# Moving the sample part of an RWKV-7 recurrence into the last round of its prompt part

## What is computed

```python
def step(S, inp):
    r_t, d_t, k_t, v_t, kk_t, b_t = inp
    sk = jnp.einsum('bhvk,bhk->bhv', S, kk_t)
    S = S * d_t[:, :, None, :] - sk[..., None] * b_t[:, :, None, :] + v_t[..., None] * k_t[:, :, None, :]
    return S, jnp.einsum('bhvk,bhk->bhv', S, r_t)
...
sT, y = lax.scan(step, s0.astype(f32), ...)
```

## Time and profile before

| | us |
|---|---|
| median of 3 runs | 4527.35 (4520.64 to 4532.71) |
| the profiled execution | 4527.17 |
| its span, first to last instruction | 4525.6 |

### The profile page before, as it was taken

How to read it: one execution, slowest core, us unless ns; L and a number is a source line. 1 busy time by engine, 2 the same in 40 slices (tenths; PEclk the granted TensorE clock), 3 DMA queues, 4 the chain that set the end, 5 groups by cost and what they waited for, 6 DMA issues and landing times. The chain is left out here.

```text
span 4525.6 us, 85734 instructions
## 1 busy us (share of the span) xinstructions
PE 4238.1 (94%) x32575; PEld 3841.0 (85%) x32575; DVE 3222.4 (71%) x6005; ACT 1430.4 (32%) x2183; POOL 1565.4 (35%) x1316
## 2 busy tenths in 40 slices
PE   7989998998777998999999998999999999999997
PEld 4888887887654987978888887999999999999996
DVE  5631334554655236899995664999999999999997
ACT  2211322111545123233336775222222222222223
POOL 6333334554022110034442332443434343443430
PEclk9999999998767999999999999999999999999998
DMA  4655665455352321134444445999999999999994
GB/s 170 204 185 191 207 231 185 178 202 169 94 172 81 89 112 52 38 104 145 142 144 158 179 172 189 344 302 299 302 298 302 302 300 302 300 302 298 304 298 156
DMA packets 523006, 928.01 MB, mean 205 GB/s; under 512 B 284032, under 2 KB 351232, under 8 KB 518688
## 3 DMA queue, kind: packets, MB, share of 16 engines
q1 hardware_dynamic: 387024, 549.29, 37.0%
q0 software_dynamic: 80960, 346.96, 22.4%
q10 hardware_dynamic: 54816, 28.85, 2.2%
HBM read 785.79 MB, written 206.30 MB: 219 GB/s over the span
## 5 line engine op out<-in xcount | busy, mean ns | idle before, releaser
L3258 POOL DMA_INDIRECT ex_rows<-expert_rows,ex_here x512 | 585.7, 1144 | 950.4 <-DVE acc_tok L3393 860.6
L3393 DVE SCALAR_TENSOR_TENSOR acc_tok<-ex_rows,ex_wsp,acc_tok 128x1024 f32<-128x1024 f32 x512 | 633.6, 1278 | 0.0
L2637 PE MATMUL ex_psa<-x_dense_high,eg_u_high 128*128 128x288 f32 x2048 | 604.4, 295 | 13.9 <-DVEq L3447 13.9
L2728 POOL TENSOR_TENSOR eg_u_low<-eg_u,eg_u_high 128x1024 fp32r<-128x1024 f32 x130 | 329.1, 2532 | 807.8 <-ACT eg_u_high L2723 807.8
L2637 PE MATMUL ex_psa<-x_dense_low,eg_u_high 128*128 128x288 f32 x2048 | 604.4, 295 | 0.0
L2637 PE MATMUL ex_psa<-x_dense_high,eg_u_low 128*128 128x288 f32 x2048 | 604.0, 295 | 0.0
L3290 PE MATMUL ex_pso<-ex_w_high,ex_v_high 128*128 128x288 f32 x2048 | 441.2, 297 | 9.7 <-DVE acc L3375 7.8
L3290 PE MATMUL ex_pso<-ex_w_high,ex_v_low 128*128 128x288 f32 x2048 | 439.9, 297 | 0.0
L3290 PE MATMUL ex_pso<-ex_w_low,ex_v_high 128*128 128x288 f32 x2048 | 438.6, 296 | 0.0
L3321 ACT ACTIVATE ex_w<-ex_psa 128x288 f32<-128x288 f32 x256 | 105.2, 411 | 1054.6 <-PE ex_psa L2637 1054.5
L3375 DVE TENSOR_TENSOR acc<-ex_pso,acc 128x576 f32<-128x576 f32 x512 | 373.8, 750 | 47.1 <-PE ex_pso L3290 47.1
(11 more groups left out here) (528 smaller groups left out, 9602.3 us busy)
## 6 DMA issues: line engine op xcount, KB each, us to landing
eg_u<-in_u SPq DMA_DIRECT2D x256, 512.0 KB, 5.4
expert_rows<-in_v SPq DMA_DIRECT2D x128, 512.0 KB, 7.0
ex_v<-in_v SPq DMA_DIRECT2D x128, 512.0 KB, 6.6
weights<-wt_stage SPq DMA_DIRECT2D x9, 4096.0 KB, 12.2
ex_g<-weights SPq DMA_DIRECT2D x128, 288.0 KB, 7.0
expert_rows<-eg_act SPq DMA_DIRECT2D x256, 128.0 KB, 1.7
proj<-in_out POOLq DMA_DIRECT2D x50, 548.5 KB, 6.2
in_w<-in_w_in SPq DMA_DIRECT2D x50, 512.0 KB, 4.7
```

The costliest lines, as they stand in the source:

```text
L2637: yield nc.tensor.matmul(out[:, 0:b - a], w[:, kc, :], half[:, kc, a:b], start=n == 0, stop=n == len(passes) - 1)
L2728: self.k.nc.gpsimd.tensor_tensor(self.ul[par][:, :, :], self.u[par % 2][:, :, :], self.uh[par][:, :, :].bitcast(F32), ALU.subtract).then_i ...
L3258: pool.indirect_dma_start(rows[i][:, :], None, table, index(here[par][:, t, j:j + 1]), element_offset=ROW_RUNS[t][0]).then_inc(s_row[i], 16)
L3393: v.scalar_tensor_tensor(out=acc_tok[:, t, :], in0=rows[i][:, at:at + D], scalar=wsp[:, i:i + 1], in1=acc_tok[:, t, :], op0=ALU.mult, op1= ...
```

## The change

`phase_rw_samples` is gone. Its work is split over the last round of `phase_rw_prompt` and what stands behind it in the same block:

- The matrix part of the sample chunk takes the place of "the next round's matrix parts" in the last round, on TensorE, ScalarE and VectorE. It uses the banks of `rwc_ps` that a chunk 0 uses and the buffers of the chunk set that the last round leaves free.
- The masking of the inputs is cut in 4 instructions of 128 x 1024, one after each piece of VectorE (`sample_inputs_masked`), with a semaphore of its own.
- The sample's state part follows the last round on each engine. In y, the product with the states comes first and the wait for u stands in the first head only; the mask of the values (half of `um`) is made ahead of rhs, and `um` lies over the conditioning weights' buffers.
- The last round's conditioning matmuls now wait for the sample chunk's `t0` step, since it shares their bank.
- One block boundary and its waits for stores are gone; two small VectorE instructions (L161 in the rows, the scaled gains) stand behind the sample part.

```diff
+class RwSampleBuffers:
...
+        self.chunk, self.ps, self.rhs, self.u = chunk, b.ps, b.rhs, b.u
...
+        self.y = ctx.enter_context(k.nc.sbuf_tensor("rws_y", [P, NPAIR, CL], F32))
+        self.kr = ctx.enter_context(k.nc.sbuf_tensor("rws_kr", [P, 2 * NPAIR, NSEQ, CL], F32))
...
+        bs = RwSampleBuffers(k, ctx, b, b.sets[R % 2][0], levels)
+        um = nc.alloc_sbuf_tensor_at("rws_um", [P, 2, NPAIR, NSEQ, CL], dtype=F32, offset=ada_at)
+        KR_PIECES = 4
+        BANK_YS, SBANK = 2, (0, 1, 3, 4)
...
+                sp.wait_ge(bs.AC.sem, bs.AC.done("y_0"))
+                sp.dma_start(io["rw_y"][NCH], bs.y[:, :, :]).then_inc(s_out, 16)
+                sp.wait_ge(bs.DV.sem, bs.DV.done("s_0"))
+                sp.dma_start(io["wkv_out"][1:NCOND].rearrange("s p a v -> p s a v"), rws.S[:, :, :, :]).then_inc(s_out, 16)
...
                         else:
                             since(pe, DS, "mod_1", r - 1)
-                            since(pe, DV, "t0_1", min(r + 1, R - 1))
+                            if r + 1 < R:
+                                since(pe, DV, "t0_1", r + 1)
+                            else:
+                                pe.wait_ge(bs.DV.sem, bs.DV.done("t0_0"))
...
+                def sample_matrix_part():
+                    pe.wait_ge(rws.s_in, 32)
+                    since(pe, AS, "y_1", R - 2)
+                    since(pe, DS, "mod_1", R - 2)
+                    since(pe, AC, f"mx{LEVELS - 1}_1", R - 1)
+                    since(pe, DV, f"t{LEVELS - 1}_1", R - 1)
+                    yield from rw_matrix_pe(k, bs, bs.chunk, rws.in5, levels, wait_of(pe))
+
+                def sample_state_part():
...
+                    at(bs.AC, "tok")
+                    pe.wait_ge(bs.s_kr, KR_PIECES)
...
+                    mm.then_inc(*bs.PE.inc("u_0"))
+                    pe.wait_ge(DS.sem, DS.done("mod_1", R - 1))
+                    for p_, rows in heads:
+                        o_ = four(BANK_YS)[rows, p_, :]
+                        for s in range(NSEQ):
+                            nc.tensor.matmul(o_, St[rows, s, p_, :], kr[rows, NPAIR + p_, s, :], start=s == 0, stop=False)
+                        nc.tensor.matmul(o_, ch.tok[rows, 2, p_, :], ch.mt[rows, p_, 192:256], start=False, stop=False)
+                        if p_ == 0 and rows.start == 0:
+                            at(bs.AC, "u")
...
                 for r in range(R):
-                    in_turn([state_part(r)] + (matrix_parts(r + 1) if r + 1 < R else []))
+                    in_turn([state_part(r)] + (matrix_parts(r + 1) if r + 1 < R else [sample_matrix_part()]))
+                sample_state_part()
...
+                def sample_inputs_masked():
+                    dve.wait_ge(rws.s_in, 32)
+                    n = 2 * NPAIR // KR_PIECES
...
+                    for i in range(0, 2 * NPAIR, n):
+                        v.tensor_tensor(bs.kr[:, i:i + n, :, :], bc(src[:, i:i + n], [P, n, NSEQ, CL]),
+                                        bc(k.seq_cols[:, :, :].unsqueeze(1), [P, n, NSEQ, CL]), ALU.mult).then_inc(bs.s_kr, 1)
+                        yield
...
-def phase_rw_samples(k, rws):
...
-                v.tensor_tensor(kr[:, :, :, :], bc(src, [P, 2 * NPAIR, NSEQ, CL]),
-                                bc(k.seq_cols[:, :, :].unsqueeze(1), [P, 2 * NPAIR, NSEQ, CL]),
-                                ALU.mult).then_inc(*DV.inc("masked_0"))
...
                 phase_rw_prompt(k, rws, ssd)
-                phase_rw_samples(k, rws)
```

More of the change, by code:

```diff
@@ L1156, in __init__ @@
         self.DV = Progress(k.sem(f"{tag}_dve"), *in_turn_steps(chunks, ["mt", "t0", "xy0"], [["t", "xy"]], levels), *each(after_dve))
+class RwSampleBuffers:
+    def __init__(self, k, ctx, b, chunk, levels):
+        self.chunk, self.ps, self.rhs, self.u = chunk, b.ps, b.rhs, b.u
+        after = lambda *steps: [f"{s}_0" for s in steps]
+        self.PE = Progress(k.sem("rws_pe"), *in_turn_steps((0,), ["mt", "m", "tok"], [["mx"], ["xmx"]], levels),
+                           *after("rhs", "u", "y", "s"))
+        self.AC = Progress(k.sem("rws_act"), *in_turn_steps((0,), ["tok"], [["mx"]], levels), *after("u", "y"))
+        self.DV = Progress(k.sem("rws_dve"), *in_turn_steps((0,), ["mt", "t0", "xy0"], [["t", "xy"]], levels),
+                           *after("rhs", "umask", "s_add", "s"))
+        self.s_kr = k.sem("rws_inputs_masked")
+        self.y = ctx.enter_context(k.nc.sbuf_tensor("rws_y", [P, NPAIR, CL], F32))
+        self.kr = ctx.enter_context(k.nc.sbuf_tensor("rws_kr", [P, 2 * NPAIR, NSEQ, CL], F32))
 class RwSampleInput:
@@ L1237, in phase_rw_prompt @@
         R = NCH // 2
+        levels = DSEQ.bit_length() - 1
+        bs = RwSampleBuffers(k, ctx, b, b.sets[R % 2][0], levels)
+        um = nc.alloc_sbuf_tensor_at("rws_um", [P, 2, NPAIR, NSEQ, CL], dtype=F32, offset=ada_at)
+        KR_PIECES = 4
+        BANK_YS, SBANK = 2, (0, 1, 3, 4)
+        s_out = k.sem("rws_stored")
+        wait_of = lambda eng: (lambda S_, step: eng.wait_ge(S_.sem, S_.done(step)))
         def at_of(eng, r):
@@ new lines, in sample_state_part @@
+                def sample_state_part():
+                    ch, St = bs.chunk, rws.S
+                    at = lambda S_, step: dve.wait_ge(S_.sem, S_.done(f"{step}_0"))
+                    rows_of = bc(k.seq_rows[:, :].unsqueeze(1).unsqueeze(3), [P, NPAIR, NSEQ, CL])
+                    dve.wait_ge(DS.sem, DS.done("mod_1", R - 1))
+                    at(bs.AC, "tok")
+                    v.tensor_tensor(um[:, 1], bc(ch.tok[:, 2, :, :].unsqueeze(2), [P, NPAIR, NSEQ, CL]), rows_of, ALU.mult)
+                    at(bs.PE, "rhs")
+                    v.tensor_copy(bs.rhs[:, :, :], four(BANK_U)).then_inc(*bs.DV.inc("rhs_0"))
+                    at(bs.AC, "u")
+                    v.tensor_tensor(um[:, 0], bc(bs.u[:, :, :].unsqueeze(2), [P, NPAIR, NSEQ, CL]), rows_of,
+                                    ALU.mult).then_inc(*bs.DV.inc("umask_0"))
+                    at(bs.PE, "s")
+                    for p_ in range(NPAIR):
+                        last = v.tensor_tensor(St[:, :, p_, :], b.ps[:, SBANK[p_], :].rearrange("p (s t) -> p s t", s=NSEQ),
+                                               St[:, :, p_, :], ALU.add)
+                    last.then_inc(*bs.DV.inc("s_add_0"))
+                    at(bs.DV, "s_add")
+                    for p_ in range(NPAIR):
+                        last = v.tensor_tensor(St[:, :, p_, :], St[:, :, p_, :],
+                                               bc(k.lam_end[:, p_, NCH:NCH + NSEQ].unsqueeze(2), [P, NSEQ, CL]), ALU.mult)
+                    last.then_inc(*bs.DV.inc("s_0"))
@@ L1453, in _ @@
+                sample_parts = lambda: [rw_matrix_dve(k, bs, bs.chunk, 1, levels, wait_of(dve)), sample_inputs_masked()]
                 in_turn(matrix_parts(0))
                 for r in range(R):
[L1455 removed]
+                    in_turn([state_part(r)] + (matrix_parts(r + 1) if r + 1 < R else sample_parts()))
+                sample_state_part()
                 dve.wait_ge(DS.sem, DS.done("mod_1", R - 1))
```

126 lines of the change are left out of this document (33 added, 93 removed).

## The result

| | before | after |
|---|---|---|
| median, one session | 4525.44 us (5 runs) | 4487.48 us (5 runs, 4481.52 to 4497.46) |
| ratio | | 0.9927, 95% interval 0.9909 to 0.9945 |
| median, a second chip | 4518.62 us (32 runs, 4496.24 to 4533.42) | 4489.18 us (9 runs, 4481.1 to 4500.45) |
| ratio | | 0.9943, 0.9924 to 0.9961 |
| span of the profiled execution | 4525.6 us | 4485.9 us |

The kernel became faster by 0.6 to 0.7%, clearly more than 0.3%, the least that can be told from no change. The forecast of 4510 and its range from 4500 to 4518 are both missed, on the fast side.

A forecast was written before the change was run, and what follows sets the result against it. It took the way from the prompt's last round to the Mamba-2 block as what counts, since everything behind starts at a block boundary. 19.97 - 5.7 + 0.6 + 2.1 = 17.0 us off 4527.35 gave 4510, range 4500 to 4518.

The forecast's parts named there:

- Removed, 19.97 us: Boundary, inverse and masking leave the path between the last round's matmuls and the sample's rhs: 19.97 us saved.
- Added, 5.7 us: Sample inverse and masking pieces put into the last round lengthen it by 5.7 us, 4 to 12 at the ends.
- The head: First piece of the sample's inverse, between rhs and the conditioning matmuls of the last round: 3.0 us added.
- The levels: The inverse's levels, matmuls on TensorE in the last round, with 0.3 of wait for a mask: 2.2 us added.
- the second rhs: In the last round, VectorE does a level and a masking piece before copying the second rhs: 0.55 us added.
- rival C: A single chunk's uncovered waits and masking pieces stretched beside GpSimd: 11.0 us saved, 4516; chance 0.22.
- rival D: Slower: pauses drop the clock to 1.2 GHz through the last round, 24.7 against 20.6 us removed, 4531; chance 0.02.
- The second half stays at 1.2 GHz, the pause before the second u gets no shorter: Last round from u on: clock left as it was, so no saving counted there.
- The clock, 2.1 us: The sample's rhs starts at 2.4 GHz and keeps it for about 3 us only: 2.1 us saved.
- the 0.6 for y's wait: In the sample part, y's first matmuls no longer wait for u's copy: 0.6 us saved.
- rival B: The clock holds at 2.4 GHz through the sample's rhs and y: 26 us saved, 4501; chance 0.18.
- Which stretch falls on which side of a clock change may move by a microsecond or two: Phases behind the edit start as before relative to the change, shifting by only a microsecond or two.

The follow-up runs named there:

- again: The kernel before, or the changed kernel, run once more unchanged for a second trace; medians 4519.25 us (before) and 4489.18 us (changed).
- x11: The kernel before with two more zeroings of `sp_state` ahead of the Mamba-2 prompt part; 4515.64 us, ratio 1.0000 to the kernel before.
- x12: The kernel before with five more zeroings of `sp_state` ahead of the Mamba-2 prompt part; 4517.63 us, ratio 1.0004 to the kernel before.
- x9: The changed kernel with two more zeroings of `sp_state` ahead of the Mamba-2 prompt part; 4488.76 us, ratio 0.9940 to the kernel before.
- x10: The changed kernel with five more zeroings of `sp_state` ahead of the Mamba-2 prompt part; 4491.78 us, ratio 0.9939 to the kernel before.
- x7: The changed kernel with the wait for the sample states' store moved into the Mamba-2 block; 4487.01 us, ratio 0.9940 to the kernel before.
- x4: The changed kernel with the sample's inverse and masks behind the last round, not interleaved with it; 4510.43 us, ratio 0.9989 to the kernel before.
- x2: The kernel before with seven unused dense matmuls while TensorE waits for the masked inputs; 4510.38 us, ratio 0.9985 to the kernel before.
- x3: The kernel before with its masks cut in four and made beside the sample's inverse; 4509.83 us, ratio 0.9973 to the kernel before.
- x1: The changed kernel with the four masks made behind the last round, so TensorE pauses before rhs; 4508.69 us, ratio 0.9982 to the kernel before.
- x8: As x7, plus eight unused dense matmuls behind the sample states' matmuls; 4486.15 us, ratio 0.9932 to the kernel before.

## Why the prediction was wrong, step by step

The direction, the place and most terms held. Four sections of the way, in the first pair of traces.

- **Removed, 19.97 us: right.** The rhs matmuls start as the turning ones end; "under 1 us" of pause is none.
- **Added, 5.7 us: right.** From the last rhs group of the round's first half to the second u it takes 1100.61 - 1084.09 = 16.5 us, where it took 1094.13 - 1083.00 = 11.1: 5.4 added. The head, rhs to conditioning matmul, is 1088.83 - 1084.09 = 4.74 against 2.02, 2.7 more (I had 3.0). The levels and the second rhs are the other 2.7 (2.2 + 0.55). Over the four traces of each order (before, again, x11, x12; after, again, x9, x10) 6.7 us are added, still within 1.0 of the term. VectorE does copy the second rhs right behind a masking piece. The stretching of a piece beside GpSimd came, 2.03 instead of 1.2, in a piece that nobody waits for; rival C, with 11.7 us of additions, falls. In x7 the clock fell within the head (the first u took 1.16), and the round took 28.0 us, as in rival D but for a short time.
- **Two slips in the working of the additions.** The range's lower end of 4 us is not worked out, as both choices were already at their lower ends, and of the 3.8 us of idle TensorE only 2.9 lie between the inverse's matmuls, the rest behind its last.
- **"The second half stays at 1.2 GHz, the pause before the second u gets no shorter": wrong.** The pause became longer, 1.48 us, and the half ran at 2.4 GHz all the same. From the second u to the end of the turning matmuls it takes 1107.5 - 1100.6 = 6.9 us instead of 1103.89 - 1094.13 = 9.8: 2.9 that I left out. The reason given was no good: I took one pause for the cause of the drop. The order of the last round is that of before in x4, x11 and x12 too, and there the same group, behind the same pause, holds the clock. Here are the lines of x4 and of x11:

```profile
1091.61 0.68 PE L1361 MATMUL rwc_ps<-rwc_rhs,rwc_xy 64*64 64x64 f32 x16 [0.52 <-DVE rwc_rhs L1513]
```
```profile
1095.75 0.68 PE L1332 MATMUL rwc_ps<-rwc_rhs,rwc_xy 64*64 64x64 f32 x16 [0.52 <-DVE rwc_rhs L1431]
```

  In before, again, x2 and x3 it takes 0.94 to 1.12. So with the old order the drop comes and goes from one execution to the next; in all seven traces with the new one it stays away (0.68). On the mean of four traces each, the second half takes 7.0 instead of 8.1 us, so 1.1 of the 2.9 are left. In this pair the round took 23.4 us against 20.9, not the 25 to 28 of the prediction. The round itself began 1.1 us later in this trace (1084.09 against 1083.00). rhs therefore moved by 16.4 us instead of 19.97 - 5.7 = 14.3.
- **The clock, 2.1 us: the step that failed.** "By 1342.43 the group takes 1.68, so the clock fell about 3 us after the first one began": that was read from thin matmuls of 128 x 8 and put on matmuls of 64 x 64. Of those, rows 1 had shown only that they don't raise the clock, not that they lose it. From the first rhs matmul to the start of the Mamba-2 block it takes 33.9 us instead of 47.6, so 13.7 came where I had 2.1 + 0.6. Of the 13.7, rhs brings 5.5, y 6.2, the way between them 1.2 (the 0.6 for y's wait among it) and what follows y 0.8. x1 and x2 switch this part off and on alone. Over the four traces of each order it is 48.4 against 33.9: 14.5 us.

Together, for this pair: 2.1 + 11.0 = 13.1, the gap from 17.0 to 30.1.

This is rival B, to which I gave 0.18: its two prices, 5.4 and 5.8, were measured as 5.5 and 6.2, and "if rhs takes about 7.7 instead of 13 us, B is right" decides it. Against B I had set only rows 7, of another kind of matmul. The nearest row should have been a 64 x 64 group that starts at the higher clock, as in the head of the inverse. Even B gave 4501, above the measured time. Its start, 4527.35, was the median of three runs only: over 32, 34 and 19 later runs the kernel before had 4518.62, 4518.92 and 4515.53. Of the 21 us between 4510 and the 4489.18 of the second session, some 9 are this start and 12 the working.

The Trainium skill, page "TensorE: Matmul & The Clock Gate", section "Part 1: The HAM clock gate (the "warmup" mystery)", was right for after, where it says that under sustained matmuls TensorE is at 2.4 GHz. It is not right for before, x1, x3 and x4: there TensorE was busy for 13.0 and some 14 us with the same matmuls and stayed at 1.2 GHz.

"**Which stretch falls on which side of a clock change may move by a microsecond or two**": wrong in size. The one later stretch varies by 13.3 us between executions. It gave the first trace of after 13.3 us that either kernel can have. Taken over the four traces of each kernel's order up to there (before, again, x11, x12; after, again, x9, x10), the Mamba-2 start is at 1170.5 and 1138.9 on average, 31.6 us apart, of which 2.2 lie ahead of the stretch that the change touches. From the round on it takes 87.7 and 58.3: 29.4 us, and the medians of the second session differ by 29.4 too. That is what the change is worth; the 38 us of the first session hold some luck.

What stays open: what makes the clock fall in one execution and not in the next, with the same order and the same waits, in the old last round and in the stand-alone inverse; and what sets the length of the later stretch.

## What to carry to other kernels

When a dependent chain of small matmuls follows other TensorE work, ask at which clock the chain begins: here it kept its level for some 23 us, so the 3 to 7 us of pause ahead of it (x4, x1), or a level lost just before it without such a pause (x3), cost another 13. Judge a type of matmul by a stretch of that type at both levels; that it never raised the clock says nothing on whether it holds it. And before a gain far behind the edit is put down to the edit, run both kernels again with a harmless disturbance: the same phase was 133 to 147 us long in the kernel before, with a few zeroings ahead of it or none. The starting time too wants more than three runs.

## What the runs showed of the hardware

- Matmuls of 64 x 64, one head after the other on the same half of the array: 27 us of nearly unbroken work left the granted clock at 0.50 (before, x1, x3, x4); the same instructions begun at 1.00 held it for 7.0 and 7.8 us of starts and through the states' matmuls behind them (after, x2). In all fourteen traces rhs and y ran at the level at which rhs began (7.0 and 7.8, or 12.5 and 14.0 us of starts). Which property counts, their size, their type or their place on the array, was not tested.
- The same group of matmuls behind the same wait of 0.52 us took 1.12 us in one execution and 0.68 in another (second u of the last round: before and again, x11 and x12).
- With the same instructions, a later phase has a mean granted clock of 0.64 to 0.71 and takes 133.1 to 146.7 us, from one execution to the next. It makes most of this kernel's spread (4494 to 4533 us over the 66 runs of the kernel before in two sessions) plausible; that it makes it was not measured run by run.
- A VectorE instruction of 128 x 1024 took 2.02 to 2.03 us beside GpSimd's work (first masking piece of after, again, x8, x9, x10) and 1.22 without; in x7, where the same piece began 0.5 us after GpSimd was done, it took 1.21.
